# Expert sums added straight into the residual, one pass for two norms, merges in pairs, attention maps counted one by one

## The reference

```python
# chunk_gated_delta, chunks of 64 tokens, for 8 heads and 2 directions
lmat  = tril(k_beta @ k.T * decay, -1) + I
sol   = triangular_solve(lmat, [v_beta, k_beta * exp(gcum)])
# ec_moe: 16 experts, each takes its 64 best tokens
xs  = u[idx]
ys  = (silu(xs @ w_gate) * (xs @ w_up)) @ w_down * gates
out = zeros.at[idx].add(ys)
h   = h + gt_f * out                     # gt_f: one number per channel
x   = rmsnorm(h, final_g)                # end of the first block
```

```python
hn   = rms_norm(x, norm_g)
proj = hn @ w_in                          # even layer
w    = softmax(q1 @ k1.T) - lam * softmax(q2 @ k2.T)   # differential attention: 4 heads, two maps each
oa   = w @ va                             # then 4 heads of attention with a forget bias, one map each
h    = x + mixed @ w_out                  # mixed: both kinds of heads, times silu(z)
h    = h + (p @ w_ple) * sigmoid(h @ w_gate)            # then an odd layer
```

## Time and profile before

| | us |
|---|---|
| median of 3 runs | 2661.61 (2658.05 to 2663.24) |
| the profiled execution | 2665.51 |
| its span | 2663.7 |
| PE (TensorE matmul) busy | 2317.9 |
| DVE (vector engine) busy | 1006.9 |
| ACT (ScalarE) busy | 623.3 |
| POOL (GpSimd) busy | 244.0 |

### The profile page before, as it was taken

How to read it: one execution, slowest core, us unless ns; L and a number is a source line. 1 busy time by engine, 2 the same in 40 slices (tenths; PEclk the granted TensorE clock), 3 DMA queues, 4 the chain that set the end, 5 groups by cost and what they waited for, 6 DMA issues and landing times. The chain is left out here.

```text
span 2663.7 us, 30068 instructions
## 1 busy us (share of the span) xinstructions
PE 2317.9 (87%) x11868; PEld 1522.0 (57%) x11868; DVE 1006.9 (38%) x1774; ACT 623.3 (23%) x1307; POOL 244.0 (9%) x279
## 2 busy tenths in 40 slices
PE   4999987599786898988989899985998889799998
PEld 2877657489764333333334333334775677688775
DVE  3667515535743011101101011106834644573453
ACT  4432314144421110110101011002322421223311
POOL 4223326600110000000000000000000000000000
PEclk8999988599887999999999999997998999899999
DMA  6123646354306999999999999994220131222130
GB/s 220 57 89 107 208 138 181 77 147 116 143 33 254 415 416 416 418 417 418 417 417 418 417 416 416 416 376 145 80 68 28 32 119 63 103 93 64 32 135 32
DMA packets 209225, 569.92 MB, mean 214 GB/s; under 512 B 62584, under 2 KB 97377, under 8 KB 175713
## 3 DMA queue, kind: packets, MB, share of 16 engines
q1 hardware_dynamic: 202104, 559.45, 55.3%
q0 software_dynamic: 2496, 8.40, 1.0%
q10 hardware_dynamic: 4521, 0.64, 0.1%
HBM read 540.14 MB, written 28.31 MB: 213 GB/s over the span
## 5 line engine op out<-in xcount | busy, mean ns | idle before, releaser
L1814 PE MATMUL ps_gate_up<-expert_ring,pair_columns 128*64 128x512 f32 x1024 | 477.5, 623 | 88.5 <-DMA expert_ring<-in_moe_w_up_dram 78.7
L1815 PE MATMUL ps_gate_up<-expert_ring,pair_columns 128*64 128x512 f32 x1024 | 479.0, 624 | 0.0
L1814 PEld LDWEIGHTS ps_gate_up<-expert_ring,pair_columns 128*64 128x64 f32 x1024 | 142.1, 143 | 379.7 <-issue 379.7
L1996 DVE TENSOR_TENSOR hidden_tokens<-silu_gate,ps_gate_up 64x512 f32<-64x512 f32 x64 | 42.5, 690 | 591.5 <-ACT silu_gate L1929 591.0
L1802 PE MATMUL ps_down<-expert_ring,hidden_columns 128*64 128x512 f32 x512 | 226.6, 595 | 0.0
L1801 PE MATMUL ps_down<-expert_ring,hidden_columns 128*64 128x512 f32 x512 | 226.6, 595 | 0.0
L1815 PEld LDWEIGHTS ps_gate_up<-expert_ring,pair_columns 128*64 128x64 f32 x1024 | 142.0, 143 | 0.0
L1801 PEld LDWEIGHTS ps_down<-expert_ring,hidden_columns 128*64 128x64 f32 x512 | 67.5, 137 | 130.1 <-issue 127.6
L846 DVE SCALAR_TENSOR_TENSOR conv_out<-conv_in,tap_columns,conv_out 128x770 f32<-128x770 f32 (+1 forms) x96 | 124.4, 1295 | 3.4
L120 PE MATMUL even_bank<-stream_high,columns_high 128*128 128x512 f32 x256 | 108.7, 425 | 3.1 <-DVE columns_low L2502 3.1
L110 DVE CAST stream_high<-stream_raw 128x2048 fp32r<-128x2048 f32 x48 | 58.6, 1221 | 138.9 <-PE out_bank L122 51.8
(11 more groups left out here) (509 smaller groups left out, 4333.1 us busy)
## 6 DMA issues: line engine op xcount, KB each, us to landing
expert_ring<-in_moe_w_gate_dram SPq DMA_DIRECT2D x64, 2048.0 KB, 18.2
expert_ring<-in_moe_w_up_dram SPq DMA_DIRECT2D x64, 2048.0 KB, 22.5
expert_ring<-in_moe_w_down_dram SPq DMA_DIRECT2D x64, 2048.0 KB, 18.1
win_ring<-in_gdn_w_in_dram SPq DMA_DIRECT2D x16, 1024.0 KB, 7.9
late_mod_ring<-in_w_mod_dram SPq DMA_DIRECT2D x16, 1024.0 KB, 5.5
stream_raw<-in_w_in_even_dram SPq DMA_DIRECT2D x16, 1024.0 KB, 5.2
stream_raw<-in_w_in_odd_dram SPq DMA_DIRECT2D x16, 1024.0 KB, 5.3
stream_raw<-in_w_ple_gate_dram SPq DMA_DIRECT2D x8, 1024.0 KB, 5.1
```

What stands on the lines that cost most here:

```text
L1814: mm(psA[LO, c], xe[:, e, k], ex.gate_up[s0][:, j, cols], start=(k == 0), stop=(k == KC - 1))
L1815: last = mm(psA[HI, c], xe[:, e, k], ex.gate_up[s1][:, j, cols], start=(k == 0), stop=(k == KC - 1))
L1996: nc.vector.tensor_tensor(hid[HI, c % 2], sg[HI, c % 2], psA[HI, c], ALU.mult).then_inc(hidden, 1)
```

## The change

It has four parts.

1. **Merges in pairs.** Units 0 and 1, then 2 and 3, go through the chain together, part by part (`product32(0)`, `product32(1)`, `merge32(0)`, ...). Units 1 and 3 get banks 4 and 5. All four are done ahead of the loop, so the loop's first step no longer holds the end of unit 3. The vector engine serves them after rows 16, 17, 26 and 27. SP issues `inputs(0, d)` right behind `scatter(0, d)`, for d = 0 and then for d = 1.
2. **Experts.** The vector engine writes `ys = psD * gate_ffn` in place of ScalarE's copies; jobs are added to `h`. `total` and its zeroing go; GpSimd clears the 128x512 tile `pair_back` in place of it. `final_g` is loaded behind the ring's first fill.
3. **Norms.** In the last pair the vector engine also makes `scaled = h * final_g` per tile, and ScalarE squares both `h` and `scaled`. From the two sums follow the final norm and the norm of the even layer (`final_norms`), by small operations on 128x4. The block `combine` goes. The even layer loads `final_g` again as SP's first transfer, makes `xn = h * norm * final_g` at once, and later, behind the mask's rounding, `h = h * norm * final_g`. SP's store of `h` waits for that (`h_normed`), and SP's further weight loads stand behind the store.
4. **Counts per map.** `scored`, `maxed` and `exped` count every map. `scores(n)` of the first map waits only for the first exponential of item n - 1, and so on through the three engines.

```diff
-        psC, qS, aN, ps32, psX = bank[0:4], bank[4], bank[5], bank[6], bank[7]
+        psC, qS, aN = bank[0:4], bank[4], bank[5]
+        merge_bank = lambda y: (bank[4], bank[5]) if y in (1, 3) else (bank[6], bank[7])
...
                 for d in DIRS:
                     scatter(0, d)
-                for d in DIRS:
                     inputs(0, d)
...
-                    if y:
-                        pe.wait_ge(w_ready, y)
+                    if y == 1:
+                        pe.wait_ge(decays, len(PIECES))
+                    elif y:
+                        pe.wait_ge(w_ready, y if y >= 4 else y - 1)
...
-                for y in range(3):
-                    product32(y)
-                    merge32(y)
-                    product64(y)
-                    merge64(y)
-                product32(3)
+                for pair in ((0, 1), (2, 3)):
+                    for part in (product32, merge32, product64, merge64):
+                        for y in pair:
+                            part(y)
...
-                for y in range(3):
-                    keep32(y)
-                    keep64(y)
-                    fill64(y)
-                keep32(3)
+                for pair in ((0, 1), (2, 3)):
+                    for part in (keep32, keep64, fill64):
+                        for y in pair:
+                            part(y)
...
-                MERGED_AFTER = {14: 0, 23: 1, 30: 2}
+                MERGED_AFTER = {16: 0, 17: 1, 26: 2, 27: 3}
...
                 ex.fill(sp, parted)
+                sp.dma_start(fg[:, :], dram["final_g"]...broadcast_to([P, D])).then_inc(fg_loaded, 16)
                 ex.keep_full(sp)
...
-                pool.wait_ge(logits, 1)
-                nc.gpsimd.memset(total, 0.0).then_inc(combined, JOBS)
+                nc.gpsimd.memset(pair_back[:, :], 0.0).then_inc(combined, JOBS)
...
-                        act.wait_ge(downed, (at + 2) * DOWN)
-                        rows = slice(e * CAP, (e + 1) * CAP)
-                        act.wait_ge(combined, (g + 1) * JOBS)
-                        act.wait_ge(stored, 2)
-                        nc.scalar.activation(ys[rows, 0:COLS], psD[LO, e], ACT.Copy)
-                        nc.scalar.activation(ys[rows, COLS:D], psD[HI, e], ACT.Copy).then_inc(stored, 1)
...
+                flat = [x[:, :, :].rearrange("p a n -> p (a n)") for x in (xs, hid)]
+                for t in range(LT):
+                    act.wait_ge(added, DONE + 2 * t + 2)
+                    ...
+                    nc.scalar.activation(flat[0], h[:, t], ACT.Square, accum_out=fs[:, 0, t:t + 1]).then_inc(summed, 1)
+                    act.wait_ge(fg_applied, t + 1)
+                    ...
+                    nc.scalar.activation(flat[1], scaled[:, t], ACT.Square, accum_out=fs[:, 1, t:t + 1]).then_inc(summed, 1)
+                act.wait_ge(summed, 2 * LT)
+                nc.scalar.activation(fs[:, 2], fs[:, 0], ACT.Sqrt, ...).then_inc(rooted, 1)
+                act.wait_ge(ratio, 1)
+                nc.scalar.activation(fs[:, 4], fs[:, 3], ACT.Sqrt, ...).then_inc(rooted, 1)
...
+                        rows = slice(e * CAP, (e + 1) * CAP)
+                        dve.wait_ge(downed, (at + 2) * DOWN)
+                        dve.wait_ge(combined, (g + 1) * JOBS)
+                        nc.vector.tensor_tensor(ys[rows, 0:COLS], psD[LO, e], gate[LO, 0:COLS], ALU.mult)
+                        nc.vector.tensor_tensor(ys[rows, COLS:D], psD[HI, e], gate[HI, COLS:D], ALU.mult).then_inc(stored, 1)
                     for j in range(JOBS):
...
-                        nc.vector.tensor_tensor(total[:, t, c], total[:, t, c], psA[:, j % CHUNKS], ALU.add).then_inc(added, 1)
+                        nc.vector.tensor_tensor(h[:, t, c], h[:, t, c], psA[:, j % CHUNKS], ALU.add).then_inc(added, 1)
+                        if not more and j % 2:
+                            dve.wait_ge(fg_loaded, 16)
+                            dve.wait_ge(added, DONE + j + 1)
+                            nc.vector.tensor_tensor(scaled[:, t], h[:, t], fg[:, :], ALU.mult).then_inc(fg_applied, 1)
...
-def combine(nc, dram, per, total):
+                seq(nc.vector.reciprocal(norms[:, 0], fs[:, 2]))
+                seq(nc.vector.tensor_tensor(fs[:, 3], fs[:, 1], norms[:, 0], ALU.mult))
+                nc.vector.tensor_tensor(fs[:, 3], fs[:, 3], norms[:, 0], ALU.mult).then_inc(ratio, 1)
+                dve.wait_ge(rooted, 2)
+                seq(nc.vector.reciprocal(norms[:, 1], fs[:, 4]))
+                nc.vector.tensor_tensor(norms[:, 1], norms[:, 1], norms[:, 0], ALU.mult)
...
-                if G0 == 0:
+                if even:
+                    sp.dma_start(fg, dram["final_g"]...broadcast_to([P, D])).then_inc(fg_loaded, 16)
                     for g in range(stream.SLOTS):
                         stream.load(sp, g)
...
+                if even:
+                    sp.wait_ge(h_normed, LT)
                 sp.dma_start(h_dram, h[:, :, :]).then_inc(h_stored, 16)
...
                     for a in range(maps):
+                        if maps == 2 and n:
+                            pe.wait_ge(exped, upto(n - 2) + a + 1)
...
-                    last.then_inc(scored, 1)
+                        last.then_inc(scored, 1)
...
-                for t in range(LT):
-                    ...
-                    nc.scalar.activation(xsq[:, t % 2], h[:, t], ACT.Square, accum_out=nss[:, 0, t:t + 1]).then_inc(squared_x, 1)
...
+                if even:
+                    dve.wait_ge(fg_loaded, 16)
+                    for t in range(LT):
+                        nc.vector.scalar_tensor_tensor(out=xn[:, t], in0=h[:, t], scalar=norms[:, 1, t:t + 1], in1=fg,
+                                                       op0=ALU.mult, op1=ALU.mult).then_inc(xnormed, 1)
...
                 if even:
+                    dve.wait_ge(xnormed, LT)
+                    for t in range(LT):
+                        nc.vector.scalar_tensor_tensor(out=h[:, t], in0=h[:, t], scalar=norms[:, 0, t:t + 1], in1=fg,
+                                                       op0=ALU.mult, op1=ALU.mult).then_inc(h_normed, 1)
```

More of the change, by code:

```diff
@@ L1125, in merge32 @@
                     for h in range(Q):
-                        last = mm(psX[:, h], P5s[y % 2][:, h], Wd[d][:, h0 + h], start=True, stop=True)
+                        last = mm(merge_bank(y)[1][:, h], P5s[y % 2][:, h], Wd[d][:, h0 + h], start=True, stop=True)
                     last.then_inc(x2, 1)
@@ L1465, in _ @@
                     remainder(x)
-                    merged(y - 1)
+                    if g:
+                        merged(y - 1)
                     remainder(x + 1)
@@ L1716, in route_and_experts @@
     scale, bias, ident = per["ffn_scale"], per["modT"][:, 0, 3 * KC:4 * KC], per["ident"]
+    h, gate, norms = per["h"], per["gate_ffn"], per["final_norms"]
     with Mem(nc) as m:
+        fg = m.sb("final_g_rows", [P, D])
+        fs = m.sb("final_small", [P, 5, LT])
         aff = m.sb("affinity", [P, LT, EXPERTS])
@@ L1952, in _ @@
                 seq = Chain(dve, chain).step
-                nc.vector.memset(pair_back[:, 0:1], 0.0).then_inc(taken, GROUPS)
+                nc.vector.memset(fs[:, :, :], 0.0).then_inc(taken, GROUPS)
                 nc.vector.memset(ys[:, :], 0.0).then_inc(added, 4)
@@ L2138, in layer_tokens @@
     biased = lambda n: even and n >= GI
+    upto = lambda n: sum(MAPS[gi] for gi, _, _ in ITEMS[:n + 1])
     SQUARE_AT, REDUCE_AT, ROOT_AT, SCALE_AT, MIX_AT = 20, 21, 25, 26, 27
@@ L2149, in layer_tokens @@
         xn, xsq = view(0, 4 * D, "p (t d) -> p t d", t=LT), view(4 * D, 2 * D, "p (i d) -> p i d", i=2)
+        fg, norms = work[:, 4 * D:5 * D], per["final_norms"]
         stage = [view(i * 2 * D, 2 * D, "p (t c) -> p t c", t=LT) for i in range(2)]
@@ L2563, in gate @@
                     nc.vector.tensor_tensor(out[g][:, hh], out[g][:, hh], z[:, g, :, hh * P:(hh + 1) * P], ALU.mult).then_inc(mixed, 1)
-                dve.wait_ge(rooted_x, 1)
-                seq(nc.vector.reciprocal(nss[:, 2], nss[:, 1]))
-                for t in range(LT):
-                    nc.vector.tensor_scalar(xn[:, t], h[:, t], nss[:, 2, t:t + 1], None, ALU.mult).then_inc(xnormed, 1)
+                if even:
[3 more added lines that the diff above has]
+                                                       op0=ALU.mult, op1=ALU.mult).then_inc(xnormed, 1)
+                else:
+                    dve.wait_ge(rooted_x, 1)
+                    seq(nc.vector.reciprocal(nss[:, 2], nss[:, 1]))
+                    for t in range(LT):
+                        nc.vector.tensor_scalar(xn[:, t], h[:, t], nss[:, 2, t:t + 1], None, ALU.mult).then_inc(xnormed, 1)
                 if G0 == 0:
```

133 lines of the change are left out of this document (56 added, 77 removed).

## The result

| | before | after |
|---|---|---|
| median, us | 2661.07 (2658.05 to 2663.24, 4 runs) | 2599.56 (2596.76 to 2602.9, 4 runs) |
| the profiled execution, us | 2665.51 | 2596.76 |
| its span, us | 2663.7 | 2595.0 |
| mean granted clock | 0.931 | 0.945 |

The ratio is 0.9771, 95% interval 0.9757 to 0.9786: 61.5 us less by the medians, 68.7 by the two spans. The forecast was 26.2 us less.

A forecast was written before the change was run, and what follows sets the result against it. Weight transfers were taken to bound the experts' stage, TensorE's order and waits the rest. 11.1 + 8.8 + 6.3 = 26.2 less than 2665.5 gives 2639.3, and 3.9 less for the median: 2635, range 2619 to 2648.

The forecast's parts named there:

- Part 2: Experts' stage: multiplies moved from ScalarE to the vector engine lie under the weight transfers, 0 us, +0.2 after the last pair.
- Part 1: Recurrence's start: merges in pairs fill the hand-overs, so unit 4 begins at 514.7 in place of 525.8, 11.1 us less.
- the loop's slow start of 8 us: Recurrence loop's first step: TensorE's stretch at 0.50 clock from 526 to 534, kept as long as before.
- the clock rival: Merges and two-map items: fewer gaps keep 2.4 GHz longer, 7 to 14 us more, about 2624; chance 0.23.
- Part 3: Norms between experts and even layer: even layer begins 9.8 us earlier, its `xn` path 1.0 later, 8.8 us less.
- The cover for the norm of `h`: Even layer: the 4.87 us norm falls into the vector engine's 5.97 us wait for TensorE; otherwise slip up to 4.9.
- the fourth weights: Even layer: the load behind SP's store of `h` goes at 28.7 us, lands by 37, wanted at 40.7; no wait.
- Part 4: Even attention: counts per map cut TensorE's 9.6 us of waits for exponentials, 6.3 us less, bounds 3 and 9.6.
- Half of the merges: Recurrence's start: something other than the chain sets it, the merges give 3 to 5 us, time about 2643; chance 0.18.
- the starved stream: Even layer: the fourth weight load, behind the store of `h`, comes too late, time above 2661.6; chance 0.02.
- nothing measurable: Whole kernel: all gains are taken back by the clock falling elsewhere, time above 2656; chance 0.05.

The follow-up runs named there:

- norms_same_places: The kernel before with parts 2 and 3 alone, plus 224 unused bytes so later tiles keep their starts modulo 256 bytes: 2652.58 us, ratio 0.9978.
- ring_up32: The kernel before with an unused tile of 32 bytes per partition ahead of the expert ring, which then starts at byte 90368: 2637.5 us, ratio 0.9903.
- ring_up288: The kernel before with 288 unused bytes ahead of the expert ring, which then starts at 90624, the next multiple of 256: 2638.94 us, ratio 0.9933.
- merges_alone: The kernel before with part 1 alone (pairs, banks, order of scatter and loads): 2646.79 us, ratio 0.9939.
- ring_half: The kernel before with 160 unused bytes ahead of the expert ring, which then starts 128 bytes above a multiple of 256: 2658.75 us, ratio 0.9997.
- counts_alone: The kernel before with part 4 alone (counts per map): 2644.53 us, ratio 0.9924.
- merges_old_queue: The kernel before with part 1 alone but SP's old order, both scatters ahead of both sets of input loads: 2642.53 us, ratio 0.9931.
- unit1_early: The kernel before with the vector engine serving merges after rows 14, 19 and 26 in place of 14, 23 and 30: 2652.36 us, ratio 0.9978.
- after_rows22: The kernel after with the vector engine serving merges of units 2 and 3 after rows 22 and 23, not 26 and 27: 2596.81 us, ratio 0.9749.

## Why the prediction was right in sign and short in size

**Part 2, the step that failed.** The prediction said "All of it lies under the transfers: 0", and that the experts' "start simply moves". The instructions of part 2 do cost nothing (norms_same_places: 950.8 us at the old place). What failed is the premise under it, that 417 GB/s is what the transfers give. I read the DMA share of 1.02 as a limit and never asked what the rate hangs on, and I passed over the diff's line with the new tile. That line alone is worth 20.7 us in the two traces. Some 2 us of this belong to the one execution of before: the stage took 949.4 to 951.1 us in the other kernels at 417 or 418 GB/s with no products added in front. By whole runs it is 26 us (22 to 30) in ring_up32 and 18 (12 to 24) in ring_up288. The sign that was set down for it, a stage that changes its length by over 2 us, is what led to it.

**Part 1, mis-sized: 11.1 forecast, 18.3 in the traces, 16.2 by merges_alone.** The mechanism was right: pairs fill the hand-overs, and the rows of the vector engine set when units 2 and 3 are served. Unit 4 began 16.9 us earlier, where 11.1 had been set down. Counted from the first `product32`, it came after 26.8 us, not 30.2, and these 3.4 us are the term that was too small: `merged(2)` came 20.9 us after the first product (at 502.98), not 24.2 (508.7). The first pair ended after 9.7 us, not 14.9, at 2.4 GHz, so the vector engine was back in its rows sooner. The sum had also put row 17 behind `merged(1)`, but by `MERGED_AFTER` it lies between `merged(0)` and `merged(1)`, where it ran; that made the forecast 1.6 us too late.

Of the other 2.4 us of unit 4's start, 1.7 are inputs that came earlier behind the row sums, which I had held unmoved. SP's order explains little of it: this stretch is 28.9 to 29.8 us in the kernels with pairs and the new order, 29.2 to 30.0 with pairs and the old order, and 29.9 to 30.8 without pairs. Its cause stays open.

The loop's 2.1 us are not the pairs' work. The prediction kept the loop's slow start of 8 us, and in after it lasted 4. But in seven other kernels with unpaired merges, in front of which no products are added, it also lasted 3 to 4 us, and their loop takes 184.2 to 184.8 us, like after's 184.7. Only before and ring_half have 9 us of it and 186.6 to 186.8. The clock in counts_alone, with the old merges, 3.7 us after unit 4's start at 531.28:

```profile
535.00:543.00 8.00, 6.97 (x72) 6.45 (x69) 1.48 (x3) 6.21 (x22) 0.00 (x0) 1.00 0.33 90
```

So the 18.3 us are near the clock rival's 17 in part by luck. Of the 7.2 above the forecast, 3.4 come through the first pair's clock and the sum's mistake with row 17, 1.7 are the earlier inputs, and 2.1 are the loop. The clock also fell again, as the windows show, so the rival's reason, fewer gaps, is only half of it. In merges_old_queue, where the second pair's inputs are there in time, it was at 0.50 from 496.1 to 499.5 all the same, so the wait for inputs is not needed for the fall. In nine profiled kernels with one unit at a time and no extra products every unit ran at 1.2 GHz (unit1_early and all the ring tests among them). Of eight with pairs and no extra products, seven were at 2.4 GHz within some 5 us of the first product. The eighth (after_rows22) took 16.5 us, without a gap.

The Trainium skill ("TensorE: Matmul & The Clock Gate", What's actually happening) has sustained activity release the throttle. The seven kernels agree; the eighth, which worked without a gap as long as it was slow, shows that the instant can't be planned on.

**Part 3, right: 8.8 forecast, 8.4 measured.** The even layer began 19.47 us after the last down product started, in place of 29.27: 9.8, as forecast. Its first projection product came 1.3 us later from the start, not 1.0, since the vector engine had `final_g` 4.05 us after its issue, not 3.7. The cover for the norm of `h` held. SP's store went at 1800.20, 26.5 us into the layer, where 26.4 was forecast, and no wait for the fourth weights followed.

**Part 4, mis-sized: 6.3 forecast, 11.9 in the traces.** The waits fell from 9.6 to 3.0 us, 6.6 less, as the sum had it. The other 5 are the clock, which the sum left as it was. The time that the 32 items spent at the lower level follows from the granted clock (twice what is missing to 1, times the length of the window): 27.4 us before and 17.1 after. At half speed, half of the difference is lost: 5.1 us, an estimate. counts_alone shows that it comes with the counts: 13.7 us at the lower level there, and 27.2 in norms_same_places, 30.7 in ring_up32, which keep the old counts. The odd layer's 2.9 come with the counts too (129.8 or 129.9 in every kernel with them, 131.2 to 132.8 in those without): the clock of its first 6 us is 1.00 in counts_alone and 0.50 in before. Why a change in the even layer's waits does that a layer later is not settled.

**The rest, 9.4 us,** is the odd layer's 2.9, which come with the counts, and 6.5 in stretches that the change doesn't touch. The 3.4 in front of the experts are the profiled execution of before: ring_up32 and ring_half have 128.4 and 128.1 there with the old code, after has 128.5. These 3.4, the loop's 2.1 and some 2 of the experts' 20.7 belong to the one profiled execution of before, which explains why the spans differ by 68.7 and the medians by 61.5.

**The rivals.** Clock: right in part 4, where it gave 5.6 us over the sum; in part 1 right in size, but less than half of its 7 us came through the clock. Half of the merges, the starved stream, nothing measurable: none came. No rival held the 21 us of the ring, and the range's lower end at 2619 missed by 19.

## What to carry to other kernels

A tile added anywhere moves all that stand above it. Compare the start addresses of the large DMA targets before and after, as part of reading a diff. Where transfers set a stage, ask for GB/s, not for the busy share, and try the ring at a multiple of 256 bytes per partition. When one trace of each kernel is compared, look at the unchanged stretches of the other runs too: a stretch with the same code in it differed by 2 to 4 us between executions here. When an engine's own serial work (here the 31 rows) sets a date, making its partners faster or serving them earlier only moves the wait.

## What the runs showed of the hardware that was not expected

A ring whose start lies 32, 64, 128 or 224 bytes above a multiple of 256 took weights at 417 to 418 GB/s, one at a multiple at 426, 2% more, with rows of 4 and 8 KB per partition and the DMA share at 1.02 in each case. The Trainium skill ("DMA: Bandwidth & Descriptors", How a descriptor splits into AXI transactions) says that a descriptor which does not start at a multiple of 256 bytes gets a first transaction that starts at the boundary of 256 bytes below it, and that the unused bytes still cost beats. The need for 256, and not 64, agrees. Counted in beats of 32 bytes, an estimate from that section, the loss would grow with the distance, with seven wasted beats at 224 and one at 32, and it does not: the runs show the same loss at 32 as at 224. Counted in transactions, another estimate from that section, a row of 4 or 8 KB takes one more at every distance, which would fit a constant loss. What exactly is paid per packet was not found; no run here tells.

The first product of the merges began anywhere from 478 to 490 us in the profiled executions without added products, with nearly the same code in front of it. Behind that point most unchanged stretches repeated within about 1 us, but not all: the output and routing took 127.9 to 128.7 us in every such kernel but before (131.9), and the way from the even projection to the first scores 141.2 to 145.5. Stage lengths told apart what medians of whole runs could not, but only where several traces agreed.
